# The running maxima of two attentions: from a product with diagonal tiles to rows of the key product

## The chip, the cores and the metric

The kernel runs on one core of one Trainium2 chip. The metric is the device time of one execution in microseconds (us), as the median of several. The core has five engines that run their own instruction streams and meet at semaphores: TensorE (PE; weight loads are listed apart as PEld), VectorE (DVE), ScalarE (ACT), GpSimd (POOL) and SyncE (SP), which here issues the DMAs.

## The reference

A batch of one sequence of 256 positions, width 1024, all in float32, passes through two blocks. The first block is a "native sparse attention" mixer (nsa) and then a block attention mixer (moba); the second is a feed forward, a mixer of two further attentions, and a feed forward. The change touches only the first two attentions. Cut to them:

```python
q = partial_rope(rms_norm(q.reshape(B, S, 16, 64), q_g), cos, sin)      # 16 heads, 4 key groups
# nsa: one compressed branch over 15 short keys, and at this length two full causal branches
p_slc = masked_softmax(q . ks * 64**-0.5, causal)       # branch 0
p_win = masked_softmax(q . kw * 64**-0.5, causal)       # branch 1
o = gate0 * o_cmp + gate1 * (p_slc @ vs) + gate2 * (p_win @ vw)
# moba: one full causal branch
p = masked_softmax(q . k * 64**-0.5, causal);  o = p @ v
x = x + gate * ((o * silu(z)) @ w_out)

def masked_softmax(s, mask):
    s = jnp.where(mask, s, -jnp.inf)
    m = jnp.max(s, axis=-1, keepdims=True)
    e = jnp.exp(s - m)
    return e / jnp.sum(e, axis=-1, keepdims=True)
```

## The kernel before

**Layout.** Positions stand in two tiles of 128 (TT = 2). Float32 operands of TensorE are split in two parts of the faster fp32r type, a rounded one and its remainder: weights as w_hi and w_lo (ACT rounds, L1105; DVE takes the remainder, L1673), activations as h_hi and h_lo, queries and keys too. `qs` holds for each of the 16 heads the rounded query in one half of the 128 partitions and the query's remainder in the other half (64 rows each). `kh` holds the rounded keys in both halves, and `kl` the keys' remainder in the half where the rounded query lies, with zeros in the other half; so kh and kl, each multiplied with the whole of qs, give the split product. Matrices `kh`, `kl` are indexed by key group g and branch br.

**Weights.** Some 300 units of weights of 512 KB stream through a ring of seven tiles w_raw. SP issues them in one fixed order (`fetch`), each when its ring tile is free: after DVE's w_lo for a weight that is split, after POOL's sum for a unit of the adaptive norm (`ada`, scaled by ACT in `scale_chunk`, summed by POOL at L2548).

**The stages around the change.** For nsa, and again for moba: the projections to q and k; heads normed, turned and rotated; then the projections z0 and z1 (`linear`, four units each), between whose units TensorE also computes the scores in their natural orientation (`maxima_scores`), and DVE takes their row maxima (`maxima`, L1814) into `mx`, one number per position, head and branch. Then comes `pair_attention`, which is written on every engine as one loop over slots: eight slots in nsa (two heads, both branches), four in moba (four heads). A slot has two items x = 0, 1, and each item has two halves, j = 0 (the first 128 keys, 2 x 256 query columns) and j = 1 (the last 128 keys, 2 x 128 columns). For each half `turned_scores` makes the transposed scores in a PSUM bank with four products (L680 twice: kh, kl; L682: the causal mask; L684: the maxima). ACT takes the exponentials (L1256 for j = 0, L1259 for j = 1); `values` multiplies them with the values (L703, L705, L707); DVE scales the results by the inverse sums in `evict` (L1827 to L1841 in nsa, L1846 and L1849 in moba).

**The maxima before the change.** Since the scores are transposed, a maximum belongs to a column, and it is subtracted by a product: a tile `shifts[x]` holds for two heads and two position tiles the diagonal matrix of the maxima, and the product of `minus_r` (all -1) with it takes the right maximum from each column. The diagonal tiles are made anew for each item: by ACT in `first_shifts` for slot 0 (L1109), by DVE in `shift` (L1860) for the others, after the item of the slot before has been scored.

**TensorE's order in a slot i:** scores (i, 0); values (i-1, 1); scores (i, 1); every second slot in nsa, every slot in moba, the transposes of a finished pair into bank 0; the hook (other work put in between: further maxima_scores, products of the output projection, the column sums of ada); values (i, 0). On DVE: evict (i-1), the shifts of slot i+1, the gates, the hook.

## Time and profile before

| what | us |
|---|---|
| median of 3 runs (lowest to highest) | 894.09 (892.96 to 894.37) |
| time of the profiled execution | 895.99 |
| its span, from first to last instruction | 894.2 |
| PE busy, and its share of the span | 868.4 (97%) |
| DVE busy | 612.5 (68%) |
| ACT busy | 494.7 (55%) |
| POOL busy | 174.6 (20%) |
| mean granted TensorE clock, share of full speed | 0.998 |

PE's share of 97% says that matmuls stand close together, not that each is as short as it can be. nsa's attention lies between about 148 and 215 us of the span, moba's between about 299 and 326 us.

### The profile page before, as it was taken

The page shows a single profiled execution, that of the slowest core. Times are in us where ns is not written, and L with a number is a line of the kernel's source. Part 1 is how long each engine was busy: PE and PEld are TensorE (multiplying, and loading weights), DVE is VectorE, ACT ScalarE, POOL GpSimd, SP SyncE. Part 2 cuts the span into 40 slices and gives each one's busy share as a digit, 9 for nine tenths or more (in the row PEclk, how much of TensorE's full clock was granted, in tenths as well). Part 3 has the DMA queues.
Part 4 walks back from the last instruction along what each step waited for, and adds up shares of the span by engine and source line. Part 5 has one row for each costly group of instructions (what it writes and reads, how often), then busy time and mean ns, then how long its engine had stood idle before and what let it go on. Part 6 is the DMA issues. An engine that isn't in the chain of part 4 may idle for free.

```text
span 894.2 us, 14775 instructions
## 1 busy us (share of the span) xinstructions
PE 868.4 (97%) x5801; PEld 790.8 (88%) x5801; DVE 612.5 (68%) x976; ACT 494.7 (55%) x780; POOL 174.6 (20%) x189
## 2 busy tenths in 40 slices
PE   3899999999999999999999999999999999999998
PEld 3788899988688889999998888899999899999886
DVE  5875678877877687666665546597668666666552
ACT  3543768555657656544444546677765654444431
POOL 1016345565054520000000004271000000000000
PEclk9999999999999999999999999999999999999999
DMA  9966646456572665666666556553345566666650
GB/s 354 361 203 220 212 147 208 142 162 192 165 240 90 191 198 155 202 200 198 197 192 194 166 155 200 145 162 118 99 139 171 181 195 188 186 188 183 207 176 24
DMA packets 45844, 163.38 MB, mean 183 GB/s; under 512 B 5200, under 2 KB 5584, under 8 KB 45776
## 3 DMA queue, kind: packets, MB, share of 16 engines
q1 hardware_dynamic: 45776, 162.44, 57.4%
q8 instruction: 47, 0.77, 0.3%
q14 instruction: 21, 0.17, 0.1%
HBM read 161.37 MB, written 1.05 MB: 182 GB/s over the span
## 4 chain that ended last, share of the span: by engine, by line
PE 88%; DVE 5%; ACT 3%; DMA 2%; issue 1%; SPq 0%; POOL 0%; DVEq 0%; ACTq 0%
PE bank L518 36%; PE bank L506 34%; PE bank L533 3%; PE bank L703 2%; PE bank L865 2%; PE bank L680 2%; DVE w_lo L1673 1%; DMA x<-in_x 1%; PE bank L705 1%; PE bank L656 1%; DMA w_raw<-in_weights 1%; PE bank L613 1%; PE bank L684 1%; PE bank L759 1%; PE bank L707 1%
## 5 line engine op out<-in xcount | busy, mean ns | idle before, releaser
L1105 ACT ACTIVATE w_hi<-w_raw 128x1024 fp32r<-128x1024 f32 (+2 forms) x249 | 259.5, 1049 | 226.5 <-PE bank L518 121.1
L1673 DVE TENSOR_TENSOR w_lo<-w_raw,w_hi 128x1024 fp32r<-128x1024 f32 (+2 forms) x249 | 301.4, 1221 | 77.5 <-ACT w_hi L1105 76.9
L518 PE MATMUL bank<-h_hi,w_hi 128*128 128x256 f32 x904 | 254.6, 282 | 0.0
L518 PE MATMUL bank<-h_lo,w_hi 128*128 128x256 f32 x904 | 251.8, 279 | 0.0
L518 PE MATMUL bank<-h_hi,w_lo 128*128 128x256 f32 x904 | 251.8, 279 | 0.0
L518 PEld LDWEIGHTS bank<-h_lo,w_hi 128*128 128x128 f32 x904 | 171.4, 190 | 0.5 <-issue 0.2
L518 PEld LDWEIGHTS bank<-h_hi,w_hi 128*128 128x128 f32 x904 | 169.9, 188 | 1.0 <-issue 0.5
L518 PEld LDWEIGHTS bank<-h_hi,w_lo 128*128 128x128 f32 x904 | 169.8, 188 | 0.0
L506 PE MATMUL bank<-w_hi,h_hi 128*128 128x512 f32 (+1 forms) x240 | 96.5, 402 | 2.6 <-DVE w_lo L1673 1.9
L2548 POOL TENSOR_TENSOR ada_acc<-ada_acc,w_raw 128x512 f32<-128x512 f32 x56 | 82.2, 1468 | 68.3 <-ACT w_raw L1109 63.2
L506 PE MATMUL bank<-w_lo,h_hi 128*128 128x512 f32 (+1 forms) x240 | 94.0, 392 | 0.0
L506 PE MATMUL bank<-w_hi,h_lo 128*128 128x512 f32 (+1 forms) x240 | 74.2, 391 | 0.4 <-DVE h_lo L1705 0.4
L506 PE MATMUL bank<-w_hi,a_hi 128*128 128x512 f32 x176 | 68.6, 390 | 0.0
L506 PE MATMUL bank<-w_lo,a_hi 128*128 128x512 f32 x176 | 68.5, 389 | 0.0
L2304 DVE TENSOR_TENSOR act<-bank,rs_row 128x512 f32<-128x512 f32 x22 | 15.2, 692 | 66.9 <-PE bank L518 66.9
L506 PEld LDWEIGHTS bank<-w_hi,h_hi 128*128 128x128 f32 x240 | 45.7, 191 | 12.4 <-issue 3.6
L506 PEld LDWEIGHTS bank<-w_hi,h_lo 128*128 128x128 f32 x240 | 45.5, 191 | 10.4 <-DVE h_lo L1705 0.9
L506 PE MATMUL bank<-w_hi,a_lo 128*128 128x512 f32 x176 | 54.2, 389 | 0.0
L506 PEld LDWEIGHTS bank<-w_lo,h_hi 128*128 128x128 f32 x240 | 45.8, 191 | 8.5
L506 PEld LDWEIGHTS bank<-w_hi,a_lo 128*128 128x128 f32 x176 | 33.0, 188 | 6.9
L506 PEld LDWEIGHTS bank<-w_lo,a_hi 128*128 128x128 f32 x176 | 33.1, 188 | 6.8
L506 PEld LDWEIGHTS bank<-w_hi,a_hi 128*128 128x128 f32 x176 | 33.0, 188 | 6.7
(321 smaller groups left out, 1404.5 us busy)
## 6 DMA issues: line engine op xcount, KB each, us to landing
w_raw<-in_weights SPq DMA_DIRECT2D x298, 512.0 KB, 4.3
w_raw<-in_weights SPq DMA_DIRECT2D x4, 360.0 KB, 3.6
x<-in_x SPq DMA_DIRECT2D x1, 1024.0 KB, 9.7
gate_row<-in_gate_bias SPq DMA_DIRECT2D x2, 512.0 KB, 6.9
out<-x SPq DMA_DIRECT2D x4, 256.0 KB, 3.4
w_raw<-in_weights SPq DMA_DIRECT2D x3, 256.0 KB, 2.6
const<-in_constants SPq DMA_DIRECT2D x1, 285.5 KB, 7.1
cols<-in_columns SPq DMA_DIRECT2D x1, 208.5 KB, 2.6
```

Source lines behind the costliest of these rows:

```text
L506: mm = e.matmul(pb[t][:, 0:n], xs, (wh, wl)[p][:, kk * n:(kk + 1) * n], start=(k + kk == 0 and q == 0 and p == 0), stop=(k + kk == kts - 1 ...
L518: mm = e.matmul(o, ws[p], xs[q], start=(k + kk == 0 and i == 0 and b % 2 == 0), stop=(k + kk == kts - 1 and i == 2 and (b % 2 == 1 or b == ...
L533: mm = e.transpose(bank[0:int(np.prod(src.shape[1:])), o:o + src.shape[0]], src, ident)
L613: mm = e.matmul(bank[:, j * P:j * P + NB], r[:, kk * 256 + j * P:kk * 256 + (j + 1) * P], flat[i][:, k + kk, :], start=(k + kk == 0 and j ...
L656: mm = e.matmul(o, q, k, start=f["t"] == 1 and j == 0, stop=f["t"] == 0 and j == len(f["items"]) - 1, skip_group_check=True)
L680: e.matmul(o, k[:, g, br, j * P:(j + 1) * P], qs[:, ha:hb + 1:2, j * P:S], start=m == 0, stop=False, skip_group_check=True)
L703: mm = e.matmul(o, p[:, a * S + t * P:a * S + (t + 1) * P], v[0], start=True, stop=t == 0)
L865: mm = e.matmul(pairs[pair][t][:, 0:n], xs[q], ws[p], start=(k + kk == 0 and i == 0), stop=(k + kk == kts - 1 and i == 2))
L1105: e.activation(w_hi[i % NSPLIT][:, 0:c], raw[v % NRAW][:, 0:c], ACT.Copy).then_inc(*rounded(v))
L1673: e.tensor_tensor(w_lo[i % NSPLIT][:, 0:c], raw[v % NRAW][:, 0:c], w_hi[i % NSPLIT][:, 0:c].bitcast(F32), ALU.subtract).then_inc(*rested(v))
L2304: e.tensor_tensor(out[:, :, :], bank[:, :].rearrange("p (k t) -> p k t", k=2), row_, ALU.mult).then_inc(*done((f, n)))
L2548: e.tensor_tensor(acc, acc, raw[u % NRAW][:, kk * 512:(kk + 1) * 512], ALU.add).then_inc(*ada_summed((c, k)))
```

## The change

The maxima are no longer subtracted by a product of their own. `mx` becomes the tail of a wider tile `mx_wide` whose first 64 columns are zero, so that a transpose of a slice of it on TensorE (`maxima_turns`, two transposes each) puts the maxima as rows into partitions 64 and up of a bank, one row per head and branch. From there they are copied into tiles of doubled queries, each row multiplied by `own_row`, which is 1 in the two rows of one head and 0 elsewhere: by ACT for the first four heads (`first_maxima`), by DVE for the other three groups of four heads (`spread_maxima`). Rows 0 to 63 of such a tile are the rounded queries, brought there from qs by DMA (`double`, two DMAs of 128 KB for each group of four heads, 16 in all). `kl` now holds the remainder of the keys in its lower half for every head, and in partitions 64 to 95 the value -1 in the rows of its branch and 0 in those of the other one. So the product with kl, over 72 to 88 rows, adds the remainder and subtracts the maxima at once, and L684's product is gone.

The tiles of the doubled queries lie where h_hi and h_lo were (`qm`) and where the keys by token were (`qm_first`), so their DMAs wait in SP's queue until z1's unit 1 or 3 has been multiplied, or until the keys have been turned. The adaptive norm's columns 5 (nsa) and 10 (moba) share bank 0 with the turned maxima and wait for them; column 5 moves from hook 1 to hook 2. POOL prepares kl's rows and own_row between the ropes of nsa_q0 and the powers of nsa_q1; its first memset shrinks from kl to 128 columns.

```diff
+        doubles = ExitStack()
+        qm = sb("qm", [P, NH, S], F32R, on=doubles)
+        doubles.close()
...
+        own_row = sb("own_row", [P, NH])
+        unit_r, mask_r = (sb(n, [P, P], F32R) for n in ("unit_r", "mask_r"))
...
-        mx = sb("mx", [P, TT, NH, 2], F32R, on=mix)
+        mx_wide = sb("mx_wide", [P, TT, HD + 2 * NH], F32R, on=mix)
+        mx = mx_wide[:, :, HD:].rearrange("p t (h b) -> p t h b", b=2)
...
-        shifts = [sb(f"shifts{x_}", [P, 2, TT, P], F32R, on=mix) for x_ in range(2)]
+        qm_first = sb("qm_first", [P, 4, S], F32R, on=mix)
...
+        doubles_of = [qm_first[:, :, :], qm[:, 0:4, :], qm[:, 8:12, :], qm[:, 4:8, :]]
+        turned_maxima = {"nsa": ((0, 4, banks[1], 0), (4, 12, banks[0], 0), (12, 16, banks[0], S)),
+                         "moba": ((0, 4, banks[1], 0), (4, 16, banks[0], 0))}
+
+        def maxima_of(s, g):
+            b = max(b_ for b_, (h0, _, _, _) in enumerate(turned_maxima[s]) if h0 <= 4 * g)
+            h0, h1, bank, c0 = turned_maxima[s][b]
+            return b, slice(HD, HD + 2 * (h1 - h0)), bank[HD:HD + 2 * (h1 - h0), c0:c0 + S], 4 * g - h0
...
+            def maxima_turns(s, b, free):
+
+                h0, h1, bank, c0 = turned_maxima[s][b]
+                w.wait_ge(*m_reduced.at(last_filling(s, h1 - 1)))
+                w.wait_ge(*free)
+                w.wait_ge(*zeroed.at(4))
+                turn(bank, [(c0 + t * P, mx_wide[:, t, 2 * h0:HD + 2 * h1].bitcast(F32))
+                            for t in range(TT)]).then_inc(*mx_turned((s, b)))
...
-                w.wait_ge(*(shift_done if i else shift_first).at((s, i, x)))
+                mg = ha // 4
+                rows_ = slice(0, maxima_of(s, mg)[1].stop)
+                for at in (kl_signed.at(1), doubled[mg].at((s, 1)), mx_spread.at((s, mg)) if mg else mx_first.at(s)):
+                    w.wait_ge(*at)
                 for j, o in enumerate((oa, ob)):
                     for at in free[j]:
                         w.wait_ge(*at)
-                    for m, k in enumerate((kh, kl)):
-                        e.matmul(o, k[:, g, br, j * P:(j + 1) * P], qs[:, ha:hb + 1:2, j * P:S], start=m == 0, stop=False,
-                                 skip_group_check=True)
+                    for m, (k, q) in enumerate(((kh[:, g, br, :], qs[:, ha:hb + 1:2, j * P:S]),
+                                                (kl[rows_, g, br, :],
+                                                 doubles_of[mg][rows_, ha % 4:ha % 4 + 3:2, j * P:S]))):
+                        e.matmul(o, k[:, j * P:(j + 1) * P], q, start=m == 0, stop=False, skip_group_check=True)
                     e.matmul(o[:, :, 0:P], mask_r[:, :], bcast(unit_r[:, :].unsqueeze(1), [P, 2, P]), start=False,
-                             stop=False, skip_group_check=True)
-                    e.matmul(o, minus_r[:, :], shifts[x][:, :, j:TT, :].rearrange("p a t q -> p a (t q)"), start=False,
                              stop=True, skip_group_check=True).then_inc(*scored((s, i, x, j)))
...
+                if j == 1:
+                    maxima_turns("nsa", 0, z_done.at(("nsa_z0", 1)))
...
-                    ada_columns(5, banks[0], pc_done.at(1))
+                    maxima_turns("nsa", 1, pc_done.at(1))
+                if i == 2:
+                    ada_columns(5, banks[0], mx_spread.at(("nsa", 2)))
...
+                if i == 4:
+                    maxima_turns("nsa", 2, o_gated.at(("nsa", 0)))
...
-                            lambda pr: ada_cols.at(5 + min(pr, 2)) if pr else gate_row_done.at(5)], nsa_hook)
+                            lambda pr: (mx_spread.at(("nsa", 3)) if pr == 1 else ada_cols.at(5 + min(pr, 2))) if pr else
+                            gate_row_done.at(5)], nsa_hook)
...
+                if j == 2:
+                    maxima_turns("moba", 0, z_done.at(("moba_z0", 1)))
...
+                if i == 0:
+                    maxima_turns("moba", 1, z_done.at(("moba_z0", 1)))
                 if i == 1:
-                    ada_columns(10, banks[0], z_done.at(("moba_z0", 1)))
+                    ada_columns(10, banks[0], mx_spread.at(("moba", 3)))
...
-            def first_shifts(s):
-
-                for x_, it in enumerate(slots[s][0]["items"]):
-                    w.wait_ge(*m_reduced.at(last_filling(s, it["heads"][1])))
-                    for a, h in enumerate(it["heads"]):
-                        for t in range(TT):
-                            last = copy(shifts[x_][:, a, t, :], ident, scale=mx_read[:, t, h, it["mx"]:it["mx"] + 1])
-                    last.then_inc(*shift_first((s, 0, x_)))
+            def first_maxima(s):
+
+                b, there, src, _ = maxima_of(s, 0)
+                w.wait_ge(*rows_known.at())
+                w.wait_ge(*mx_turned.at((s, b)))
+                for h in range(4):
+                    last = copy(doubles_of[0][there, h, :], src, scale=own_row[there, h:h + 1])
+                last.then_inc(*mx_first(s))
...
+            def spread_maxima(s, g):
+
+                b, there, src, h = maxima_of(s, g)
+                for at in (rows_known.at(), mx_turned.at((s, b)), streamed.at((of[f"{s}_z1"][3 if g == 3 else 1], 1))):
+                    w.wait_ge(*at)
+                rows_ = there.stop - there.start
+                e.tensor_tensor(doubles_of[g][there, :, :], bcast(src.unsqueeze(1), [rows_, 4, S]),
+                                bcast(own_row[there, h:h + 4].unsqueeze(2), [rows_, 4, S]),
+                                ALU.mult).then_inc(*mx_spread((s, g)))
...
-                def shift(i, x_):
-
-                    it = slots[s][i]["items"][x_]
-                    (ha, hb), m = it["heads"], it["mx"]
-                    w.wait_ge(*m_reduced.at(last_filling(s, hb)))
-                    w.wait_ge(*scored.at((s, i - 1, x_, 1)))
-                    e.tensor_tensor(shifts[x_][:, :, :, :], bcast(ident.unsqueeze(1).unsqueeze(1), [P, 2, TT, P]),
-                                    bcast(mx_read[:, :, ha:hb + 1:2, m].rearrange("p t a -> p a t").unsqueeze(3),
-                                          [P, 2, TT, P]), ALU.mult).then_inc(*shift_done((s, i, x_)))
-
                 for i in range(n + 3):
                     pr = slots[s][i - 2]["close"] if 0 <= i - 2 < n else None
                     if 0 < i <= n:
                         evict(i - 1)
-                    for x_ in range(2 if i + 1 < n else 0):
-                        shift(i + 1, x_)
+                    for g in {("nsa", 1): (1, 2), ("moba", 0): (1, 2), ("moba", 1): (3,)}.get((s, i), ()):
+                        spread_maxima(s, g)
                     if 0 < i <= n:
...
-                    hi, lo = (z[here, :, br, :].rearrange("p (k i) s -> p i k s", i=2)[:, i, :, :] for z in (kh, kl))
+                    hi, lo = (z[at, :, br, :].rearrange("p (k i) s -> p i k s", i=2)[:, i, :, :]
+                              for z, at in ((kh, here), (kl, HALVES[0])))
                     w.wait_ge(*heads_rounded.at((name, br, i)))
-                    w.wait_ge(*zeroed.at(4))
...
+                if step_ == 1 and i == 4:
+                    spread_maxima("nsa", 3)
...
-                                       (tokv[:, 1, :, HD:], 1.0), (kl[:, :, :, :].bitcast(F32), 0.0))):
+                                       (tokv[:, 1, :, HD:], 1.0), (mx_wide[:, :, 0:HD].bitcast(F32), 0.0))):
...
+            e.memset(kl[HD:HD + 2 * NH, :, :, :].bitcast(F32), -1.0).then_inc(*kl_signed(0))
+            w.wait_ge(*const_in.at())
+            w.wait_ge(*eye_in.at())
+            w.wait_ge(*kl_signed.at(0))
+            z = kl[HD:HD + 2 * NH, :, :, :]
+            e.tensor_tensor(z, z.bitcast(F32), bcast(con("parity")[HD:HD + 2 * NH, :].unsqueeze(1).unsqueeze(3),
+                                                     [2 * NH, NKV, 2, S]), ALU.mult).then_inc(*kl_signed(1))
+            pairs_ = ident[HD:HD + 2 * NH, HD:HD + 2 * NH].rearrange("p (h b) -> p h b", b=2)
+            e.tensor_tensor(own_row[HD:HD + 2 * NH, :], pairs_[:, :, 0], pairs_[:, :, 1], ALU.add).then_inc(*rows_known())
+            w.wait_ge(*kl_signed.at(1))
+            w.wait_ge(*rows_known.at())
...
+            def double(s, g):
+
+                w.wait_ge(*heads_rounded.at((f"{s}_q{g // 2}", g % 2, 1)))
+                if g:
+                    w.wait_ge(*streamed.at((of[f"{s}_z1"][3 if g == 3 else 1], 1)))
+                else:
+                    w.wait_ge(*heads_turned.at(("nsa_kskw", 1) if s == "nsa" else ("moba_kv", 0)))
+                for i, here in enumerate(HALVES):
+                    e.dma_start(doubles_of[g][0:HD, i:4:2, :].bitcast(F32),
+                                qs[here, 4 * g + i:4 * g + 4:2, :].bitcast(F32)).then_inc(*doubled[g]((s, i)))
...
-            for u in range(of["nsa_q0"][0], of["moba_z0"][0]):
+            first, rest, last = of["nsa_z0"][0] + 7, of["nsa_z1"][1] + 8, of["nsa_z1"][3] + 8
+            for u in range(of["nsa_q0"][0], first):
+                fetch(u)
+            double("nsa", 0)
+            for u in range(first, rest):
+                fetch(u)
+            double("nsa", 1)
+            double("nsa", 2)
+            for u in range(rest, last):
+                fetch(u)
+            double("nsa", 3)
+            for u in range(last, of["moba_z0"][0]):
                 fetch(u)
             w.wait_ge(*y_gated.at(("nsa", 1, 1)))
...
-            for u in range(of["moba_z0"][0], len(units)):
+            first, rest, last = of["moba_z1"][0] + 7, of["moba_z1"][1] + 8, of["moba_z1"][3] + 8
+            for u in range(of["moba_z0"][0], first):
+                fetch(u)
+            double("moba", 0)
+            for u in range(first, rest):
+                fetch(u)
+            double("moba", 1)
+            double("moba", 2)
+            for u in range(rest, last):
+                fetch(u)
+            double("moba", 3)
+            for u in range(last, len(units)):
                 fetch(u)
```

## Rows read from the trace of the kernel before

**Rows 1.** The page's first part: busy time of each engine, share of the span.

```profile
PE 868.4 (97%) x5801; PEld 790.8 (88%) x5801; DVE 612.5 (68%) x976; ACT 494.7 (55%) x780; POOL 174.6 (20%) x189
```

**Rows 2.** Busy time in two stretches, nsa's and moba's attention; then clock, DMA share, GB/s.

```profile
150.00:160.00 10.00, 10.00 (x74) 9.09 (x73) 8.32 (x23) 8.59 (x18) 4.67 (x4) 1.00 0.32 99
300.00:310.00 10.00, 10.00 (x71) 8.92 (x70) 5.98 (x10) 9.22 (x18) 5.49 (x4) 1.00 0.65 203
```

**Rows 3.** Instructions on the tile shifts: shortest, median, longest in ns; first and last start.

```profile
L684 PE MATMUL bank<-shifts,minus_r x48: 274/337/401, 149.3 to 318.8; 128*128 128x512 f32 x24, 128*128 128x256 f32 x24
L1860 DVE TENSOR_TENSOR shifts<-const,mx x20: 678/694/1800, 150.2 to 314.0; 128x512 fp32r<-128x512 f32 x20
L1109 ACT ACTIVATE shifts<-const,mx x16: 386/387/403, 138.4 to 292.9; 128x128 fp32r<-128x128 f32 x16
```

**Rows 4.** PE's timeline, an item of slot 2 in nsa: start, duration, instruction.

```profile
161.75 0.40 PE L684 MATMUL bank<-shifts,minus_r 128*128 128x512 f32 x1
161.99 0.28 PE L680 MATMUL bank<-qs,kh 128*128 128x256 f32 x1
...
162.35 0.29 PE L684 MATMUL bank<-shifts,minus_r 128*128 128x256 f32 x1
162.47 0.33 PE L703 MATMUL bank<-tokv,soft_t 128*128 128x65 f32 x2
```

**Rows 5.** PE's timeline: two transposes; then column sums of ada.

```profile
107.77 0.38 PE L533 MATMUL bank<-const,gated 128*128 128x128 f32 x2
...
157.84 1.02 PE L547 MATMUL bank<-ada_acc,const 128*128 128x512 f32 x2
```

**Rows 6.** PE's timeline in nsa: slot 2 begins; slot 4, item 1, half 1.

```profile
161.06 0.50 PE L680 MATMUL bank<-qs,kh 128*128 128x512 f32 x1
...
180.42 0.39 PE L680 MATMUL bank<-qs,kh 128*128 128x256 f32 x1 [0.32 <-ACT soft_t L1259]
```

**Rows 7.** DVE's timeline in nsa around evict (0): merged where alike.

```profile
154.79 1.28 DVE L1785 SCALAR_TENSOR_TENSOR zs<-tmp,bank 128x512 f32<-128x512 f32 x2
156.68 0.25 DVE L1827 RECIPROCAL factors<-bank 128x4 f32<-128x4 f32 x2 [0.61 <-PE bank L707]
...
159.75 2.96 DVE L1860 TENSOR_TENSOR shifts<-const,mx 128x512 fp32r<-128x512 f32 x2
```

**Rows 8.** ACT's timeline in nsa: exponentials of slot 1, item 0, half 0.

```profile
155.79 0.60 ACT L1256 ACTIVATE soft_t<-bank 128x512 f32<-128x512 f32 x1
```

**Rows 9.** PE's timeline in moba: slot 0; hook 1; slot 3, item 1, half 1; out0.

```profile
299.08 0.39 PE L680 MATMUL bank<-qs,kh 128*128 128x512 f32 x1
...
307.05 1.02 PE L547 MATMUL bank<-ada_acc,const 128*128 128x512 f32 x2
...
318.35 0.34 PE L680 MATMUL bank<-qs,kh 128*128 128x256 f32 x1
...
319.77 0.47 PE L506 MATMUL bank<-w_hi,qs 128*128 128x512 f32 x1 [0.29 <-issue]
```

**Rows 10.** DVE's timeline in moba: the end of evict (0); shifts of slot 3.

```profile
306.05 0.76 DVE L1849 TENSOR_TENSOR tokq<-bank,stats 128x256 f32<-128x256 f32 x2
...
313.38 2.36 DVE L1860 TENSOR_TENSOR shifts<-const,mx 128x512 fp32r<-128x512 f32 x2
```

**Rows 11.** ACT's timeline in moba: exponentials of slots 1 and 3, item 0, half 0.

```profile
305.54 0.61 ACT L1256 ACTIVATE soft_t<-bank 128x512 f32<-128x512 f32 x1
...
317.40 0.58 ACT L1256 ACTIVATE soft_t<-bank 128x512 f32<-128x512 f32 x1
```

**Rows 12.** POOL's timeline: memset of kl; power of nsa_q1; one sum of ada.

```profile
1.58 1.80 POOL L2554 MEMSET kl<- 128x2048 f32 x1
...
92.00 0.27 POOL L2520 TENSOR_SCALAR stats<-stats 128x16 f32<-128x16 f32 x1 [3.70 <-DVE stats L1720]
92.36 2.93 POOL L2523 TENSOR_TENSOR stats<-stats 128x16 f32<-128x16 f32 x1
...
119.09 1.30 POOL L2548 TENSOR_TENSOR ada_acc<-ada_acc,w_raw 128x512 f32<-128x512 f32 x1 [13.30 <-ACT w_raw L1109]
```

**Rows 13.** DVE's timeline: heads of nsa_q1 are scaled.

```profile
99.96 1.29 DVE L1740 TENSOR_TENSOR tokq<-bank,stats 128x512 f32<-128x512 f32 x2
```

**Rows 14.** SP's timeline in moba's z1: two weights are issued.

```profile
290.40 0.80 SPq L2645 DMA_DIRECT2D w_raw<-in_weights  x2
```

**Rows 15.** The page's last part: DMAs, KB each, us from issue to landing.

```profile
const<-in_constants SPq DMA_DIRECT2D x1, 285.5 KB, 7.1
```

13 lines of the change are left out of this document (6 added, 7 removed).

## The prediction

> **What bounds the kernel now.** I read the busy shares first, then the stretches of the two attentions, then everything that touches the tile shifts, and last the timelines of PE, DVE and ACT slot by slot. PE is busy for 97% of the span [rows 1], and for all of each 10 us stretch in both attentions, at a granted clock of 1.00 [rows 2]; at full clock, nothing is to be had from it or to be lost to it. The reader is to see that work taken out of PE's stream shortens the kernel by its issue time, unless PE then comes earlier to something that another engine has not finished. ACT is the next fullest, 8.6 and 9.2 of 10 us, DVE has 8.3 in nsa and 6.0 in moba [rows 2]. So the change is worth what it takes from PE, less what PE then waits for. The rest of the span is not touched; what follows the attentions hangs on their end and moves with it.
>
> **What it takes from PE.** L684 is issued 48 times, two for each of 24 items [rows 3]. A product of 512 columns holds PE from 161.75 to 161.99, 0.24 us; one of 256 from 162.35 to 162.47, 0.12 us [rows 4]. An item loses 0.36 us, the 24 items 8.6 us. The other three products keep their columns; kl's is only cut in rows, and I take its price as unchanged.
>
> **What it adds to PE.** Ten transposes in five pairs. A pair lasts 0.38 us [rows 5]; the last 0.17 us of a duration overlaps with the next instruction (0.29 long, the next starts after 0.12 [rows 4]), so a pair costs 0.21 us, five 1.05 us. Ada's column 5 (1.02 us, 0.85 without the tail [rows 5]) only moves from hook 1 to hook 2. Without any new wait the change would give 8.6 - 1.05 = 7.6 us.
>
> **What it takes from the others.** DVE loses 20 shifts, ACT 16 diagonal copies [rows 3]. A shift takes 0.69 us as a median and 1.80 at most [rows 3]; a pair took 2.96 in slot 1 [rows 7]. ACT gets eight small copies for the sixteen, at no more than 0.39 each. They wait for the turned maxima, some 2.5 us later than the old ones began, with scaled ada units behind them that POOL sums; PE needs those sums only a hook later. I cost that at nothing; if the cover were gone it would be up to 2.5 us.
>
> **What it adds to DVE: six spreads** of 1024 elements for each partition, read from PSUM. None is in the trace. The nearest row that reads PSUM is 2 x 512 elements in 1.28 us [rows 7]; a spread is one such pair in one instruction, so 1.2 us. The other bound is the slowest shift: 1.80 for 512 elements against 0.69 [rows 3], in proportion 3.1 us. I take 1.2, since L1785 is nearer in its operands (one from PSUM, one from SBUF) and the shift reads both from SBUF. The Trainium skill (GPSIMD Engine Reference, Specifications) says that GpSimd shares its SBUF interfaces with VectorE and that they contend when a DVE instruction has two SBUF inputs. By that rule a spread, with one, stays at 1.2, and the trace agrees so far as the two rows go; if it did not hold, the result would be the third rival below.
>
> **The first new gate: slot 2 of nsa.** Its scores need group 1's spread, which DVE does after evict (0). Evict (0) began at 156.68 and took until 159.75 [rows 7], 3.07 us. It begins when values (0, 1) are done; three items fewer stand before them (1.08) and one pair of transposes more (0.21). But PE soon meets the exponentials of slot 1, which ACT began at 155.79 [rows 8] because of its own work, so I count 0.7 us: evict runs from 156.0 to 159.05, the spread to 160.25, and slot 2 starts at 160.3 instead of 161.06 [rows 6]. PE alone would be there at about 158.5 (161.06 less five items, less the moved column, plus two pairs, less the 0.3 that it waited for the old shift). So the gate swallows 1.8 us, and slot 2 is only 0.75 earlier.
>
> **The rest of nsa.** Twelve items at 0.36 give 4.3 us. The moved column comes back, 0.85, and one pair, 0.21. PE waited 0.32 for an exponential in slot 4 [rows 6]; ACT was late because DVE's gate stood behind two shifts, so this falls away: 0.3. The other spread, of group 3, is done in hook 4, two slots before it is needed. Sum after slot 2: 4.3 + 0.3 - 0.85 - 0.21 = 3.55. nsa gives 0.75 + 3.55 = 4.3 us.
>
> **moba, the second gate.** Slot 0 starts 0.2 late (a pair before it), at 299.3 [rows 9]; two items fewer and another pair later the maxima of the other twelve heads are turned at about 301.6, group 1's spread is done at 302.9, just when PE comes to slot 1. Now ada's column 10, in hook 1, waits for group 3's spread, since both use bank 0, and this spread stands behind evict (0). Evict (0) ended at 306.81 [rows 10]; one item earlier, 306.45; plus 1.2 makes 307.65. PE begins the column at 307.7 instead of 307.05 [rows 9]: 0.65 **late**. Behind it in PE's stream are the values of slot 1, and so everything.
>
> **Where moba gets it back.** Three items later (1.1 us) PE would be 0.4 ahead. But slot 3's exponentials, 317.40 [rows 11], are held by ACT's own chain of copies and roundings that hangs on slot 2, where PE is level with before; half 1 of item (3, 1) starts no earlier than at 318.35 [rows 9]. What remains is at out0: it started at 319.77 after a wait [rows 9] for DVE's remainder of the weight, which stood behind the shifts of slot 3, 2.36 us at 313.38 [rows 10]. Without them it is ready early and PE starts at about 319.1. moba gives 0.7 us.
>
> **POOL.** Before nsa_q1's power come a memset of kl's rows, 2048 elements, 1.80 us by the same length [rows 12]; a product over 2048 elements, four times a sum of 512 at 1.30 less a start of some 0.1, 4.9 us [rows 12]; and a tiny sum, 0.2. POOL was free from 88.30 (92.00 less 3.70 idle) and took 3.3 us for the power [rows 12]; now it ends at 88.3 + 6.9 + 3.3 = 98.5. DVE scales these heads at 99.96 [rows 13], so 1.4 us are left and it costs nothing. The Trainium skill (GPSIMD Engine Reference, Elementwise — side-by-side cycle accounting) measures 4497 ns for such a product of 2048 float32 elements; by it POOL would be done 0.4 us sooner.
>
> **DMAs.** Sixteen of 128 KB on SP's queue. No row has one from SBUF to SBUF; a load of 285.5 KB took 7.1 us to land [rows 15]; I take nothing as the lower bound and 7.1 as the upper. The tightest are those of moba's group 1: issued behind the weights of 290.40, 0.4 each, four until 292.8 [rows 14], landed by 300 at the upper bound, needed at 302.9. Each one waits in SP's queue, so weights wait behind it; but the waits (unit 1 or 3 of z1 multiplied) end where SP waited for ring tiles anyway, and moba's first, which waits for the turned keys, holds back one ada unit that ACT scales only beside slot 0. Cost nothing.
>
> **The sum.** 4.3 + 0.7 = 5.0 us off the profiled execution (span 894.2, its time 895.99). The median of the runs shown, 894.09, is 1.9 below the latter; I take 5.0 from the median: **889.1 us**.
>
> **The rivals.**
> 1. The gates don't bind: evict and spread overlap better than I count. 7.6 us, 886.5. For it: DVE is relieved of 20 shifts, and evicts become quicker. Against it: evict, then spread, is one chain of 4.3 us behind a product.
> 2. The spreads are dearer, 1.8 us each: slot 2 is 0.6 later; in moba groups 1 and 2 delay slot 1 by 0.6 and group 3 comes another 0.6 to 0.9 later. 5.0 - 2.1 = 2.9, 891.2.
> 3. The spreads slow down as the shifts did, 3.1 us: nsa gives 4.3 - 1.9 = 2.4. In moba two end at 307.8, evict (0) at 308.8, the third at 311.9, 4.8 behind before instead of 0.65. 5.0 - 1.9 - 4.2 = -1.1: 895.2, no change that can be measured.
> 4. The other side, slower: POOL's product over 32 partitions with repeated strides. Place: between the ropes and nsa_q1's power, then DVE, then the queries of all nsa. From 6.3 us on (4.9 + 1.4) it is on the path; from 6.3 + 5.0 + 1.8 = 13.1 it makes the kernel measurably slower, 5 to 6 ns an element against 2.5 in the rows. Likely price if so: 15 us, 898.
>
> **How the numbers follow.** My forecast 0.52, its own range 888.0 to 890.4. Rival 1 0.18, rival 2 0.14, rival 3 0.08, rival 4 0.08. This kernel's measurement tells 0.2%, 1.8 us, from no change; so faster 0.84 (the forecast, rivals 1 and 2), same 0.08, slower 0.08. The range must hold the forecast and most of rivals 1 and 2: 886.3 to 892.2.
>
> **What would show it.** L684 gone, and scores starting a third earlier within an item; slot 2 of nsa preceded by about 1 us in which PE waits for a DVE spread; the column products in moba's hook 1 again preceded by a wait for a spread, some 1.3 us; L1785's rate in the spreads. A spread far from 1.2 us, a PE wait on a DMA of doubles, or DVE waiting for POOL near 100 us would make me wrong; so would a stage behind the attentions that waits for weights and gives the gain back.

## The result: 0.8% slower, and what the profile after shows

The changed kernel takes 901.62 us (898.46 to 902.47, 4 runs) against 894.0 us of the kernel before on the same chip (892.96 to 894.37, 4 runs): ratio 1.0081, 95% interval 1.0055 to 1.0107. I had forecast 889.1 us. One execution in all that follows, of the kernel "diagonal's product twice" (1745.31 us), ran at half rate throughout and is left out. Line numbers have moved: L518 is L534, L506 is L522, L680 is L710, L533 is L549, L547 is L563, L703 to L707 are L730 to L734; `spread_maxima` is L1859.

I laid the starts of the score products of both traces side by side and cut the span at them. The lengths in us (columns: from the first instruction to the first scores of nsa; to slot 2; to the last scores of nsa; to the first scores of moba; to the diagonal's product, L973 before and L1011 now, 72 products into feed forward 1; to the end):

| kernel | start | slots 0, 1 | slot 2 to last | to moba | moba | behind |
|---|---|---|---|---|---|---|
| before | 148.60 | 12.47 | 43.98 | 94.03 | 57.28 | 537.84 |
| changed | 145.71 | 12.22 | 43.71 | 94.65 | 57.23 | 547.09 |

The first column varies from execution to execution (144.9 to 148.6 us in the profiles below; the kernel before ran at half clock for 3.4 us, from 44.0 us on, in its own). The others repeat within 0.1 us when the same program is profiled again. So the attentions gave nothing, and 9.25 us were lost behind them, **where neither an instruction of PE nor its order had changed**. Three things are to be seen.

First, the two gates. PE's waits between 100 and 360 us (us in total, times, longest):

```profile
PE bank L710 <- DVE qm L1859: 1.4, 1, 1.4
PE bank L563 <- DVE qm L1859: 1.3, 1, 1.3
```

and DVE ahead of the first of them, then PE's scores of slot 2 (start, duration):

```profile
153.07 0.25 DVE L1874 RECIPROCAL factors<-bank 128x4 f32<-128x4 f32 x2 [2.07 <-PE bank L734]
153.36 0.98 DVE L1877 TENSOR_TENSOR factors<-factors,gates 128x4 f32<-128x4 f32 x2
154.38 1.02 DVE L1883 TENSOR_TENSOR parts_of_o<-bank,factors 128x384 f32<-128x384 f32 x2
155.44 1.09 DVE L1888 TENSOR_REDUCE tokq<-parts_of_o 128x128 f32<-128x384 f32 x2
156.56 2.36 DVE L1859 TENSOR_TENSOR qm<-bank,own_row 16x1024 fp32r<-16x1024 f32 x2
```

```profile
157.93 0.47 PE L710 MATMUL bank<-qs,kh 128*128 128x512 f32 x1 [1.37 <-DVE qm L1859]
...
158.96 0.33 PE L730 MATMUL bank<-tokv,soft_t 128*128 128x65 f32 x2
...
159.36 0.64 PE L730 MATMUL bank<-tokv,soft_t 128*128 128x65 f32 x2
```

Evict (0) from 153.07 to 156.53, the spread 1.2 us, PE released: the gate that I had drawn [rows 6, 7]. moba's column products wait 1.3 us.

Second, the last two rows are the same pair of products, 0.33 us long at 158.96 and 0.64 at 159.36. The stretches below say why (PE, PEld, DVE, ACT, POOL busy; then the granted clock):

```profile
145.00:155.00 10.00, 9.99 (x75) 8.92 (x74) 6.72 (x20) 8.63 (x18) 4.89 (x5) 1.00 0.65 200
159.00:166.00 7.00, 7.00 (x30) 6.07 (x29) 3.86 (x10) 1.69 (x4) 2.18 (x2) 0.52 0.51 150
300.00:310.00 10.00, 8.57 (x59) 7.33 (x58) 7.19 (x12) 7.40 (x15) 8.35 (x7) 1.00 0.84 242
```

Granted clock 0.52: PE runs at the lower of its two levels, 1.2 GHz, for 6.8 us from 159.3 on, right behind the wait. The kernel before had 1.00 in its attentions [rows 2].

Third, feed forward 1 and 2. PE is busy for all of both, at clock 1.00; what differs is how many products it gets through. Stretches of PE alone (the up products of feed forward 1, by which its input is widened; its down products; up and down products of feed forward 2), before:

```profile
357.00:467.00 110.00, 110.00 (x973) 1.00 0.64 196
469.00:503.00 34.00, 34.00 (x151) 1.00 0.60 185
715.00:830.00 115.00, 115.00 (x978) 1.00 0.63 191
832.00:890.00 58.00, 58.00 (x258) 1.00 0.42 128
```

and after:

```profile
357.00:467.00 110.00, 110.00 (x936) 1.00 0.61 187
471.00:505.00 34.00, 34.00 (x147) 1.00 0.59 179
721.00:835.00 114.00, 114.00 (x970) 1.00 0.63 191
837.00:895.00 58.00, 58.00 (x250) 1.00 0.42 127
```

936 products in 110 us where there were 973: one starts every 117.5 ns instead of 113.1. In the down products, of 512 columns, it is 231 instead of 225 ns by these rows. By the starts themselves the pace is constant over the whole stretch: 113.3 or 117.8 ns for 256 columns, 226.7 or 233.3 for 512. The up products of feed forward 2 had 117.8 before and have it still. 984 up products at 4.5 ns make 4.4 us.

One thing more shows when the starts are followed across the diagonal's product of feed forward 1. The 72 up products ahead of it started every 117.8 ns in the kernel before and start every 113.4 ns in the changed one; behind it the two paces are exchanged.

### The profile page after: what moved, and what is told of

Read it like the earlier page. It is cut to its first block, busy times and chain, and to the rows that moved or that the text cites. A ratio compares the mean times of both kernels' runs of the same rounds, so it can differ in the third digit from the quotient of the medians.

```text
span 900.6 us, 14701 instructions
## 1 busy us (share of the span) xinstructions
PE 873.8 (97%) x5763; PEld 791.9 (88%) x5763; DVE 601.5 (67%) x962; ACT 493.2 (55%) x771; POOL 176.1 (20%) x192
## 4 chain that ended last, share of the span: by engine, by line
PE 88%; DVE 5%; ACT 3%; DMA 2%; issue 1%; SPq 0%; POOL 0%; DVEq 0%; ACTq 0%
PE bank L534 37%; PE bank L522 34%; PE bank L549 3%; PE bank L894 2%; PE bank L730 2%; PE bank L710 2%; DMA x<-in_x 1%; DVE w_lo L1710 1%; PE bank L732 1%; PE bank L672 1%; PE bank L629 1%; PE bank L734 1%; DMA w_raw<-in_weights 1%; PE bank L786 1%; ACT w_hi L1143 1%
## 5 line engine op out<-in xcount | busy, mean ns | idle before, releaser
L534 PE MATMUL bank<-h_hi,w_hi 128*128 128x256 f32 x904 | 256.1, 283 | 0.0
L534 PE MATMUL bank<-h_hi,w_lo 128*128 128x256 f32 x904 | 253.3, 280 | 0.0
L534 PE MATMUL bank<-h_lo,w_hi 128*128 128x256 f32 x904 | 253.3, 280 | 0.0
L534 PEld LDWEIGHTS bank<-h_lo,w_hi 128*128 128x128 f32 x904 | 172.6, 191 | 0.6 <-issue 0.2
L534 PEld LDWEIGHTS bank<-h_hi,w_hi 128*128 128x128 f32 x904 | 169.9, 188 | 1.0 <-issue 0.6
L534 PEld LDWEIGHTS bank<-h_hi,w_lo 128*128 128x128 f32 x904 | 169.8, 188 | 0.0
L522 PE MATMUL bank<-w_hi,h_hi 128*128 128x512 f32 (+1 forms) x240 | 95.7, 399 | 1.2 <-issue 0.5
L522 PE MATMUL bank<-w_lo,h_hi 128*128 128x512 f32 (+1 forms) x240 | 93.3, 389 | 0.0
L2587 POOL TENSOR_TENSOR ada_acc<-ada_acc,w_raw 128x512 f32<-128x512 f32 x56 | 77.6, 1386 | 72.5 <-ACT w_raw L1147 67.4
L522 PE MATMUL bank<-w_hi,h_lo 128*128 128x512 f32 (+1 forms) x240 | 73.7, 388 | 0.4 <-DVE h_lo L1742 0.4
L522 PE MATMUL bank<-w_lo,a_hi 128*128 128x512 f32 x176 | 69.9, 397 | 0.0
L522 PE MATMUL bank<-w_hi,a_hi 128*128 128x512 f32 x176 | 69.3, 394 | 0.0
L522 PE MATMUL bank<-w_hi,a_lo 128*128 128x512 f32 x176 | 55.3, 395 | 0.0
L522 PEld LDWEIGHTS bank<-w_hi,h_hi 128*128 128x128 f32 x240 | 45.4, 189 | 10.7 <-issue 2.3
L522 PEld LDWEIGHTS bank<-w_hi,h_lo 128*128 128x128 f32 x240 | 45.0, 188 | 10.2 <-DVE h_lo L1742 0.9
L522 PEld LDWEIGHTS bank<-w_lo,h_hi 128*128 128x128 f32 x240 | 45.4, 189 | 8.4
L522 PEld LDWEIGHTS bank<-w_lo,a_hi 128*128 128x128 f32 x176 | 33.1, 188 | 8.2
L522 PEld LDWEIGHTS bank<-w_hi,a_lo 128*128 128x128 f32 x176 | 33.1, 188 | 8.0
L522 PEld LDWEIGHTS bank<-w_hi,a_hi 128*128 128x128 f32 x176 | 33.1, 188 | 7.5
```

The source lines that it names most:

```text
L522: mm = e.matmul(pb[t][:, 0:n], xs, (wh, wl)[p][:, kk * n:(kk + 1) * n], start=(k + kk == 0 and q == 0 and p == 0), stop=(k + kk == kts - 1 ...
L534: mm = e.matmul(o, ws[p], xs[q], start=(k + kk == 0 and i == 0 and b % 2 == 0), stop=(k + kk == kts - 1 and i == 2 and (b % 2 == 1 or b == ...
L2587: e.tensor_tensor(acc, acc, raw[u % NRAW][:, kk * 512:(kk + 1) * 512], ALU.add).then_inc(*ada_summed((c, k)))
```

## The experiments

Sixteen runs, of fourteen new kernels; two runs repeat a kernel for another profile. Ratios are to the kernel before, with 95% intervals; lengths are cut as in the table above.

**The changed kernel again.**

> The changed kernel once more, nothing altered. In its first profile three losses stand against the forecast: a wait of 1.37 us at the scores of slot 2 with 6.8 us at half the granted clock right behind it (some 3.4 us), a wait of 1.3 us in the second attention, and feed forward 1, whose 984 products of 256 columns start every 117.8 ns where the kernel before has 113.3 ns (5.2 us from the diagonal's product to the end of that feed forward, no line of it changed). Theory A: the pace of the products is a property of the program, so this run shows 117.8 ns again and a time of 898 to 903 us. Theory B: the pace is drawn anew in each execution; then this profile has about even chances of 113.3 ns in either feed forward, and the times of one kernel spread over 5 us. The clock drop may come and go: of the four timed runs, one (898.46 us) had a granted clock of 1.000, the others 0.996 to 0.998, which is the size of the drop.

902.81 us (1.0095, 1.0069 to 1.0121); behind the diagonal 547.08 us, every pace as in the first profile. Theory A holds: the pace belongs to the program. So does the wait of 1.37 us. The half clock does not always follow it: one of the four executions, 900.06 us, had a granted clock of 1.000, the rest 0.994 to 0.996.

**The spreads moved.** Group 2's spread goes to slot 2, group 3's to moba's slot 0.

```diff
+                    if (s, i) == ("nsa", 2):
+                        spread_maxima(s, 2)
...
-                    for g in {("nsa", 1): (1, 2), ("moba", 0): (1, 2), ("moba", 1): (3,)}.get((s, i), ()):
+                    for g in {("nsa", 1): (1,), ("moba", 0): (1, 2, 3)}.get((s, i), ()):
```

> The spread of heads 8 to 11 is moved behind the second round of maxima in the first attention (slot 2 needs only that of heads 4 to 7), and in the second attention the spread of heads 12 to 15 is made a slot earlier, so that the ada column of hook 1 finds it done. Theory A (the two waits and the clock drop behind the first are what kept the attentions from gaining): the wait of 1.37 us at slot 2 falls to under 0.3 us, the half clock goes, the wait of 1.3 us goes, and the kernel is 1.1 + 3.4 + 1.3 = 5.8 us faster than the changed one at the same pace of the feed forwards: about 895 to 896 us. Rival: the second attention hangs on ScalarE's exponentials and VectorE, and its 1.3 us come back as other waits: 4.5 us, 897 us. Rival: the half clock stays without the wait, or comes elsewhere: 2.4 us only. Should the pace of feed forward 1 flip to 113.3 ns because the order before it changed, 5.2 us more go, and the profile shows it.

902.13 us (1.0092, 1.0068 to 1.0115), so neither the 895 to 896 us of the theory nor the 897 of the rival. The part in moba came true: its wait is gone and moba takes 55.68 us instead of 57.23. The part in nsa was a misreading of mine: group 1's spread was first in DVE's row already, and what it waits for is evict (0); the wait stayed 1.37 us and so did the half clock.

**The old addresses.** The change had freed `minus_r` (512 bytes in each partition) and added `own_row` (64) ahead of unit_r, so every tile of the attentions, feed forwards and second mix up to the maxima moved by 448 bytes. This kernel gives own_row 512.

```diff
-        own_row = sb("own_row", [P, NH])
+        own_row = sb("own_row", [P, P])[:, 0:NH]
```

> The changed kernel with own_row allocated at 512 bytes a partition instead of 64, which puts all tiles of the feed forwards back on the addresses of the kernel before (they had moved by 448 bytes). Theory of the addresses: the products of feed forward 1 go back to 113.3 ns and the kernel is 5 us faster, 896 to 897 us. Rival (the operands of the up products, h_hi, h_lo, w_hi and w_lo, had not moved at all; what changed is what the matrix engine did before): still 117.8 ns, 901 us within 0.3%.

892.55 us (0.9984, 0.9964 to 1.0004): 10 us faster than the changed kernel, twice what the theory of the addresses had said. Behind the diagonal it takes 537.91 us, as before the change (537.84). Its stretches in the feed forwards:

```profile
357.00:465.00 108.00, 108.00 (x956) 1.00 0.63 195
467.00:500.00 33.00, 33.00 (x147) 1.00 0.62 189
```

113.0 ns again; and since the down products and the second mix come back too, the gain is 9.2 us and not 5. Its ten executions also price the half clock: 889.18 and 889.49 us at a granted clock of 1.000, 891.5 to 893.1 at 0.996 to 0.998, 895.3 to 895.8 at 0.994.

**One more wait instruction** (`e.wait_ge(*eye_in.at())` ahead of the diagonal's product).

> The changed kernel with one more wait instruction in TensorE's queue, on a semaphore long reached, ahead of the diagonal's product in feed forward 1. In both kernels it is at that product that the pace of the stream switches (before: 117.8 ns ahead of it and 113.3 ns behind it; after the change: 113.5 and 117.8). Theory of the order (the pace depends on how the instructions fall, as their count or their spacing at the switch): the pace behind the diagonal becomes 113.3 ns and the kernel 5 us faster, 896 to 897 us. Rival: an instruction that only waits has no part in it: 117.8 ns and no change, 901 us.

904.1 us (1.0105, 1.0074 to 1.0136), 547.20 us behind the diagonal: no effect on the pace. In its profile the half clock lasted 10.2 us instead of 6.8, and slot 2 to the last scores took 45.27 us.

**The kernel before, moved by 64 bytes.**

```diff
+        sb("pad", [P, 16])
         unit_r, minus_r, mask_r = (sb(n, [P, P], F32R) for n in ("unit_r", "minus_r", "mask_r"))
```

> The kernel before with nothing added but an unused tile of 64 bytes a partition ahead of unit_r, so that every tile behind it lies 64 bytes further on, which is where the change put them up to whole multiples of 512 bytes. Not one instruction differs. Theory of the addresses: the products of feed forward 1 go from 113.3 to 117.8 ns (256 columns) and from 227 to 233 ns (512 columns, both feed forwards and the products between them); with some 1.4 us in the second mix that makes 9 us: 902 to 903 us. Rival (the padded kernel was faster for another reason, its instructions' or its tiles' place relative to what the change added): no change, 894 us.

903.03 us (1.0105, 1.0089 to 1.0120). Not an instruction differs from the kernel before, and it is 9.8 us slower (903.03 against 893.25). Behind the diagonal it takes 547.11 us, the changed kernel 547.09:

```profile
357.00:467.00 110.00, 110.00 (x937) 1.00 0.61 189
472.00:505.00 33.00, 33.00 (x143) 1.00 0.59 178
```

**The diagonal's product twice.**

> The changed kernel with the product that spreads the diagonal issued twice in feed forward 1 (the second writes the same values over the first). The pace of the 256-column products switches at this product in every profile so far, though none of their operands had moved. Theory of a carried state (the product toggles something that lasts until the next such product): behind two of them the pace is 113.3 ns, and with 0.4 us for the extra product the kernel is 4.0 us faster, 897 to 898 us. Rival (the pace behind the diagonal is set by addresses that are in use there, whatever went before): 117.8 ns, and 0.4 us slower, 902 us.

902.43, 904.22 and 904.46 us (1.0114, 1.0099 to 1.0129). Its second profile:

> The kernel with the diagonal's product issued twice once more, for its profile, since the one taken of it fell in an execution whose TensorE ran at half its rate throughout. Its timed runs (902.4 to 904.5 us) already speak against a toggled state, which asked for 897 to 898 us: the profile should show 117.8 ns behind the second product too. If it shows 113.3 ns, the gain went elsewhere.

899.6 us, 117.8 ns behind both products. A state that each such product toggles is refuted. This profile has the 1.38 us wait at slot 2 and no half clock behind it (granted clock 1.00, 40.49 us from slot 2 to the last scores).

**The feed forwards' tiles moved back**, the attentions' left where the change put them (`sb("pad_ffn1", [P, 112], on=ffn1)` and the like for mix2 and ffn2).

> The changed kernel with 448 unused bytes at the head of the regions of both feed forwards and of the second mix: their tiles lie where they lay before the change, while those of the first two attentions stay moved. Theory that an operand's own address sets the pace: the down products, which read a1 and a2, go from 233 to 227 ns (1.0 us in feed forward 1, 0.7 us behind it, 1.7 us in feed forward 2); for the up products of 256 columns, whose operands never moved, the state that PE brings from the attentions decides, so they stay at 117.8 ns: 898 us. Rival: the tiles of feed forward 1 set the up products' pace as well (113.3 ns): 894 us.

898.09 us (1.0047, 1.0032 to 1.0063). The down products are back, the up products are not:

```profile
357.00:467.00 110.00, 110.00 (x936) 1.00 0.61 188
473.00:505.00 32.00, 32.00 (x143) 1.00 0.61 183
...
836.00:894.00 58.00, 58.00 (x258) 1.00 0.41 127
```

So the loss has two parts: 4.8 us that hang on the tiles of the feed forwards and the second mix themselves (547.09 to 542.27; 1.7 us in feed forward 1, 1.4 in the second mix, 1.75 in feed forward 2), and 4.4 us (to 537.84) in products none of whose operands ever moved.

**Which tile is it, then?** Both kernels start from the padded one. The first moves the attentions' tiles by 64 bytes (a pad at the head of `mix`), the second only unit_r, mask_r and lead.

> The padded kernel with 64 unused bytes at the head of the region of the first two attentions: their tiles (tokq, qs, kh, kl, tokv, zs, soft_t and those behind) lie 64 bytes off again, unit_r, mask_r, lead and all tiles of the feed forwards and the second mix stay where the kernel before has them. Theory M (the tiles of the attentions' region set the pace of the up products of feed forward 1): 117.8 ns, and with 0.3 to 0.5 us more in the attentions 5 us slower than the padded kernel, 897 to 898 us. Theory C (it is unit_r, mask_r or lead): 113.3 ns and 893 us.

> The converse: the regions of the attentions, the second mix and both feed forwards lie where the kernel before has them, and only unit_r, mask_r and lead lie 64 bytes off as in the changed kernel. Theory M: 113.3 ns in feed forward 1, 892 to 893 us. Theory C: 117.8 ns, 897 us.

897.15 us (1.0037, 1.0019 to 1.0056) and 117.8 ns; 893.1 us (0.9994, 0.9980 to 1.0007) and 113.3 ns. It is a tile of the attentions. The profile of the first brought something else: its wait for the spread is the same 1.4 us, yet the granted clock stayed at 1.00 and slot 2 to the last scores took 40.47 us, where the half clock makes 43.7. One half clock of 6.8 us costs 3.2 us.

```profile
157.00:194.00 37.00, 36.81 (x271) 1.00 0.53 160
```

Four kernels then moved ever less of that region, from the kernel "best" below; each was run once.

> The fastest kernel (885.2 us of span) with 64 unused bytes ahead of qs: tokq stays, qs, kh, kl, tokv, zs, soft_t and the rest of the attentions' region lie 64 bytes off. With tokq moved too the up products of feed forward 1 took 117.8 ns. If tokq is the tile that decides, 113.3 ns come back here; if it is one of those behind it, 117.8 ns and a span 4.4 to 5 us longer, some 890 us.

> The same 64 bytes ahead of kh: tokq and qs stay. qs holds the attentions' rounded outputs too, which the last products ahead of feed forward 1 read as their weights (they went from 227.7 to 233.3 ns when it moved). If qs decides, because it is the last moved tile that the matrix engine reads before the feed forward: 113.3 ns. If kh, kl or one behind them: 117.8 ns.

> The same 64 bytes ahead of tokv: tokq, qs, kh and kl stay, tokv, zs, soft_t and the rest move. tokv is read in rows of 65 values of 4 bytes, 260 bytes, and is the one operand whose rows are no whole number of 64 bytes. If such uneven reads leave behind what the up products inherit: 117.8 ns here and 113.3 ns with the pad ahead of zs. If qs or kh decides: 113.3 ns in both.

> The same 64 bytes ahead of zs: only zs, soft_t, mx_wide, the gates and the small tiles behind them move. soft_t is the weights' side of the products with the values. If one of these decides: 117.8 ns; if not, 113.3 ns and the time of the fastest kernel.

From qs on: 892.02 us, 542.28 us behind the diagonal. From kh, tokv or zs on: 887.12, 886.54 and 888.93 us, 537.9 us each (they differ in their start, 145.4 to 147.7 us). The up products with the pad ahead of qs, and ahead of kh:

```profile
350.00:460.00 110.00, 110.00 (x937) 1.00 0.61 189
```

```profile
350.00:458.00 108.00, 108.00 (x956) 1.00 0.63 195
```

It is qs: the two kernels differ in its address alone. It holds the attentions' rounded outputs, which the last products ahead of feed forward 1 read as their weights. Their own pace goes from 227.7 to 233.3 ns, and the up products behind them, which don't read it, have another pace than before. In all nine profiles with qs moved, the 72 up products ahead of the diagonal's product run at 113.4 ns and those behind it at 117.8; in the seven with qs at its old address ("h_128" below apart) it is 117.8 ahead and 113.3 behind.

In the kernel before, qs and the feed forwards' a1 and a2 begin at a multiple of 128 bytes, in the changed one 64 bytes past one; h_hi and h_lo lie 64 past in both. All moves here were by 64 bytes or back by 448, which is the same up to whole multiples of 512. No run moved these tiles by another amount, so a rule of 128 bytes isn't shown.

**Both waits taken away, old addresses: "best".** As the padded kernel, and:

```diff
+                        if i == 0:
+                            spread_maxima(s, 1)
                         w.wait_ge(*o_evicted.at((s, i)))
                         for t in range(TT):
                             e.reduce_sum(otok[:, t, :].rearrange("p (h d) -> p h d", d=HD)[:, h:h + 3:2, :],
...
-                    for g in {("nsa", 1): (1, 2), ("moba", 0): (1, 2), ("moba", 1): (3,)}.get((s, i), ()):
+                    for g in {("nsa", 1): (2,), ("moba", 0): (1, 2, 3)}.get((s, i), ()):
```

> The padded kernel with the two waits on spreads taken away: in the first attention the spread of heads 4 to 7 goes between the two halves of slot 0's eviction on VectorE, so that it ends 1.1 us earlier and slot 2 waits 0.3 us instead of 1.37; in the second attention the spread of heads 12 to 15 is made a slot earlier, which took 1.55 us from the second attention when it was done alone. Theory (the half clock follows on the wait of 1.37 us): with the wait nearly gone the granted clock stays at 1.00 in the first attention, 3.4 us: in all 1.1 + 3.4 + 1.55 = 6.0 us under the padded kernel, 886.5 us. Rival: the half clock comes all the same (a wait of 0.3 us, or what lies ahead of it, is enough): 889.9 us.

886.82 us (886.31 to 887.20, 5 runs), ratio 0.9924, 0.9912 to 0.9937: 0.8% faster than the kernel before. DVE, then PE at slot 2:

```profile
154.42 1.02 DVE L1883 TENSOR_TENSOR parts_of_o<-bank,factors 128x384 f32<-128x384 f32 x2
155.47 1.22 DVE L1859 TENSOR_TENSOR qm<-bank,own_row 16x1024 fp32r<-16x1024 f32 x1
156.72 1.09 DVE L1890 TENSOR_REDUCE tokq<-parts_of_o 128x128 f32<-128x384 f32 x2
```

```profile
156.84 0.47 PE L710 MATMUL bank<-qs,kh 128*128 128x512 f32 x1 [0.24 <-DVE qm L1859]
```

The wait is 0.24 us, and in none of five executions was the granted clock under 0.999. moba takes 55.46 us without its wait.

**h_hi and h_lo at a multiple of 128 bytes** (64 bytes of pad ahead of them, own_row 64 bytes shorter; the constants, diag and the other tiles between them and own_row move along).

> The fastest kernel so far (885.2 us of span) with h_hi, h_lo and what lies behind them up to ada_acc 64 bytes further on, so that h_hi and h_lo begin at a multiple of 128 bytes, as a1_hi does where the down products start every 227 ns (at 64 bytes past a multiple they start every 233 ns); the tiles from unit_r on stay. The products that read h_hi and h_lo as weights take 228.9 ns of 512 columns now. Theory (each operand wants a multiple of 128 bytes): these go to 227 ns, the up products of both feed forwards to 113.3 ns or less, feed forward 2 with them: 4.4 us and some 1 us in the projections less, 881 to 882 us. Rival (the pace of the up products depends on more than their own operands): anything from no change to both feed forwards at 117.8 ns, 887 to 892 us.

897.25 us (1.0041, 1.0029 to 1.0054). Each half of the theory went its own way. The 512-column products that read h as weights did speed up, from 228.9 to 226.7 ns. The up products, which read h as the moving side, fell to a third pace, 120.0 ns, in both feed forwards, ahead of the diagonal's product and behind it. Which of the moved tiles does that was not tried apart:

```profile
240.00:265.00 25.00, 25.00 (x112) 1.00 0.76 250
350.00:460.00 110.00, 110.00 (x919) 1.00 0.60 181
```

What the experiments did to each stage (us; "hc" marks a half clock in that stage):

| kernel | slots 0, 1 | slot 2 to last | to moba | moba | behind |
|---|---|---|---|---|---|
| before, moved by 64 bytes | 12.46 | 43.91 | 94.28 | 57.72 | 547.11 |
| spreads moved | 12.21 | 43.71 hc | 94.67 | 55.68 | 547.09 |
| padded | 12.20 | 43.65 hc | 94.49 | 56.99 | 537.91 |
| feed forwards moved back | 12.21 | 43.71 hc | 94.67 | 57.22 | 542.27 |
| mix left moved | 12.23 | 40.47 | 94.69 | 57.19 | 542.31 |
| from qs | 11.09 | 40.46 | 94.67 | 55.66 | 542.28 |
| best | 11.07 | 40.38 | 94.48 | 55.46 | 538.08 |
| h_128 | 11.08 | 40.46 | 94.12 | 55.58 | 548.07 |

## Why the prediction was wrong

The step that failed is a sentence: "The rest of the span is not touched; what follows the attentions hangs on their end and moves with it." The end of the kernel moved by +9.25 us against the diagonal's product, behind the attentions. The diff shows its cause in two allocation lines, which I quoted and priced at nothing. The account of 901.6 us: 9.8 us from the addresses (the kernel before with 64 bytes of padding), about 4 us gained in the attentions (padded, at full clock, 889.2 and 889.5 against 893.7), 3.2 us for a half clock of 6.8 us in three executions of four. That is 894.0 + 9.8 - 4.2 = 899.6 without the half clock and 902.8 with it; measured were 898.5, and 901.3 to 902.5.

None of my rivals had it. The one on the slower side was POOL's product; it took 3.59 us, less than my 4.9. The small sum took 1.19 where I had 0.2, so that the three new instructions come to 6.6 and my 6.9 was near by luck. (The 4497 ns quoted in the prediction were measured on an addition; 3.59 us is what this product takes here. And the rival's "5 to 6 ns an element" doesn't fit its own 13.1 us, which would be 6.4.)

```profile
85.42 1.80 POOL L2604 MEMSET kl<- 32x2048 f32 x1
87.39 3.59 POOL L2609 TENSOR_TENSOR kl<-kl,const 32x2048 fp32r<-32x2048 f32 x1 [0.17 <-POOL kl L2604]
90.95 1.19 POOL L2612 TENSOR_TENSOR own_row<-const 32x16 f32<-32x16 f32 x1
```

Step by step:

- **PE's item, 0.36 us: right.** The last two items of nsa start 3.17 us apart (198.47, 201.64) where they were 3.54 apart. Slot 2 to the last scores at full clock is 40.4 to 40.5 us against 43.98: 3.5 less. The forecast of 3.55 was for all twelve items; up to this cut, with the last item's products behind it, it makes 3.2.
- **The spread, 1.2 us: right** (1.211 to 1.222). The DMAs of the doubles landed in 4.0 to 6.2 us for `qm` and 2.4 to 7.4 for `qm_first`, the last a little above my bound of 7.1, and PE didn't wait for them. The ACT copies took 0.45 us each, not 0.39 at most:

```profile
L1859 DVE TENSOR_TENSOR qm<-bank,own_row x6: 1211/1222/1222, 156.6 to 303.8; 24x1024 fp32r<-24x1024 f32 x3, 16x1024 fp32r<-16x1024 f32 x2, 8x1024 fp32r<-8x1024 f32 x1
```

- **The gate at slot 2: the place right, the size 0.5 us off.** Slots 0 and 1 gave 0.25 us, not 0.75: evict (0) took 3.46 us instead of the 3.07 that I carried over. Its product of the inverse sums with the gates accounts for 0.32 of that. Before, then after:

```profile
156.25 1.28 POOL L2548 TENSOR_TENSOR ada_acc<-ada_acc,w_raw 128x512 f32<-128x512 f32 x1
156.97 0.66 DVE L1830 TENSOR_TENSOR factors<-factors,gates 128x4 f32<-128x4 f32 x2
```

```profile
152.96 1.29 POOL L2587 TENSOR_TENSOR ada_acc<-ada_acc,w_raw 128x512 f32<-128x512 f32 x1
```

  The first of these two products of four elements took 0.906 us where it had 0.582. It ended at 154.27 and POOL's sum at 154.24, before at 157.55 and 157.53. In nsa's other slots it is the same: 0.17 us when no POOL sum is under way or one is about to end, up to 0.98 otherwise, and then it ends 0.02 to 0.03 us behind the sum. Both its inputs lie in SBUF. The spread, which reads one from PSUM, took 1.21 to 1.22 us also where a POOL sum ran beside it for 1.08 of them. So evict (0) grew because it comes earlier within POOL's sum, and the third rival's slow spread did not come. Apart from that, 1.1 us of the wait came from spreading behind the reduction and not ahead of it.
- **"At full clock, nothing is to be had from it or to be lost to it": wrong, 3.2 us.** I had listed a new wait of about 1 us as a sign that I was right, and did not ask what PE's clock does behind it. Of the 56 executions with the 1.37 us wait, in ten runs, 11 stayed at 1.000 (2 of the 10 of the padded kernel, 3 of the 10 of "mix left moved"); with a wait of 0.24 us all 15 stayed at 0.999 or more, and so did the four of the kernel before moved by 64 bytes, which has no such wait. Of nine profiles with the wait, seven show the half clock, from 0 to 2.2 us behind the wait's end. That taking this wait away takes the half clock in the attentions away is shown; what decides in a given execution is not. Nor does every wait of that length do it: eight profiles have moba's wait of 1.3 us, and in none did the clock fall behind it.
- **moba, 0.7 us: too much.** 0.05 us in the changed kernel, 0.3 at the old addresses. The wait in hook 1 was as forecast (1.3 us), but it was on the path whole: without it moba takes 1.5 us less. ACT's chain, on which I had counted to absorb the difference either way, did not.
- **nsa's last scores to moba: 0.46 us longer at the old addresses, where 0.15 less was forecast.** About 0.2 is the pair of transposes ahead of moba's slot 0, as forecast. But the last item's 0.36 was not gained: the first product behind the last values (L894, before L865) started 6.84 us after the last scores, where it had 6.69. It now follows a wait of 0.30 us and starts 0.1 behind the end of DVE's remainder of the weight, which stands behind an evict whose product with the gates took 0.84 us instead of 0.67. In the padded kernel:

```profile
207.40 1.22 DVE L1710 TENSOR_TENSOR w_lo<-w_raw,w_hi 128x1024 fp32r<-128x1024 f32 x1
208.72 0.47 PE L894 MATMUL bank<-w_hi,qs 128*128 128x512 f32 x1 [0.30 <-issue]
```

With the addresses and the clock held, the forecast of 889.1 us stands beside 889.2 and 889.5, but that is in part luck. They are two executions, and the part ahead of the first scores varies by itself. By the stages (slot 2 to the last scores at full clock), the change gives 0.27 + 3.5 - 0.46 + 0.29 = 3.6 us at the old addresses, where I had 5.0: the reading of the attentions was right in kind and 1.4 us too high.

## What to carry to other kernels

A change that adds, drops or resizes a tile moves all those allocated behind it, and that alone can cost more than the change gives: pad so that the rest keeps its addresses, or run the kernel before with nothing but the padding, before judging an edit of a per cent. Where stages without a changed line take longer, count products in a stretch of equal length; a busy share of 100% and a clock of 1.00 hide it. A new wait of a microsecond on PE may cost several more behind it (here 3.2 us in most executions behind the one at slot 2, nothing behind the one in moba), so look for a place for the producer one instruction earlier on its engine first.

## What the runs showed of the hardware

- **The pace of equal products depends on addresses in steps of 64 bytes.** Products of 512 columns start every 226.7 to 227.7 ns when their weights (a1, a2, the outputs in qs) lie at a multiple of 128 bytes, every 233.3 when 64 past it; h_hi at 64 past one gives 228.9, at a multiple 226.7. Products of 256 columns have three paces, 113.3, 117.8 and 120.0 ns, each held over 984 products in a row. The Trainium skill (SBUF — State Buffer, Operand start alignment) lets an operand of 4 bytes start at any multiple of 4 and says that this is about legality, its runs having timed nothing; here the 64 bytes cost 9.8 us of 894.
- **Part of that pace depends on a tile that the products don't read.** Moving qs alone changes the up products of feed forward 1 from 113.3 to 117.8 ns, though they read h and w only. In the 72 of them ahead of the diagonal's product it is the other way round: 117.8 ns with qs in its old place and 113.4 with it moved. What is carried over, and why it changes at this product, is open: one more wait instruction, a doubled diagonal, other spreads and their order left it as it was.
- **The half clock behind a short wait.** A wait of PE of 1.37 us was followed by 6.8 us at 1.2 GHz (10.2 in one profile) in most executions (45 of 56 had a mean granted clock under 1.000) and by none in some. A wait of 1.3 us in moba was followed by none in eight profiles.
- **A small VectorE product waits for GpSimd's sum.** With both inputs in SBUF, four elements took 0.15 to 0.17 us alone and up to 0.98 beside a sum, ending 0.02 to 0.03 us behind it; the spread, with one input in PSUM, stayed at 1.21 to 1.22 us beside one.
